# Four tiles open behind a kept layer norm, its scaled chunks in SBUF, and later groups of the multilayer stages tile by tile

## The reference

```python
for i in range(DEPTH_2):                       # 2
    mix = nsa_pool_mixer(...) if i % 2 == 0 else gla_mixer(...)
    x = layer_norm(ALPHA * x + mix, ln1_g[i], ln1_b[i])
    x = layer_norm(ALPHA * x + sqrelu_mlp(x, mlp_w1[i], mlp_w2[i]), ln2_g[i], ln2_b[i])

def layer_norm(x, g, b):
    mu = mean(x); var = mean(square(x - mu))
    return (x - mu) * rsqrt(var + LN_EPS) * g + b

def sqrelu_mlp(x, w1, w2):                     # w1: 1024 x 4096, w2: 4096 x 1024
    return square(relu(x @ w1)) @ w2
```

## Time and profile before

| what | us |
|---|---|
| median of 3 runs | 1947.76 |
| the runs | 1945.41 to 1947.98 |
| the profiled execution, its own time | 1947.59 |
| span of its trace, first to last instruction | 1945.8 |

### The profile page before, as it was taken

One profiled execution on the slowest core, in us unless ns is written; L12 is line 12 of the kernel. 1 busy time (PEld: TensorE's weight loads), 2 busy tenths in 40 slices (PEclk: granted clock), 3 DMA queues, 4 the chain that ended last, 5 costly groups with the idle time before them and its releaser, 6 DMA issues.

```text
span 1945.8 us, 24354 instructions
## 1 busy us (share of the span) xinstructions
PE 1892.9 (97%) x8938; PEld 1516.6 (78%) x8938; DVE 793.7 (41%) x1305; ACT 432.0 (22%) x850; POOL 1071.2 (55%) x622
## 2 busy tenths in 40 slices
PE   7989999999999999999999999999999999999997
PEld 5868787888888888875778888887776778888885
DVE  4965333343342434579451212136523371212126
ACT  4323322310000121045140101023414140101022
POOL 5734663565757656430456665564752446666552
PEclk9989999999999999999999999999999999999998
DMA  5322332222333325210123332222321223332321
GB/s 220 109 65 74 96 102 65 78 96 87 119 98 108 98 84 208 67 55 2 56 76 107 98 97 87 87 95 79 108 87 42 67 75 99 106 99 97 97 87 44
DMA packets 46879, 175.99 MB, mean 90 GB/s; under 512 B 5200, under 2 KB 5328, under 8 KB 46032
## 3 DMA queue, kind: packets, MB, share of 16 engines
q1 hardware_dynamic: 46512, 169.55, 27.0%
q10 hardware_dynamic: 288, 5.31, 0.7%
HBM read 172.74 MB, written 2.10 MB: 90 GB/s over the span
## 4 chain that ended last, share of the span: by engine, by line
PE 94%; DVE 3%; ACT 1%; issue 1%; POOL 0%; DMA 0%; SPq 0%; DVEq 0%; POOLq 0%
PE acc L471 17%; PE acc L473 17%; PE acc L472 17%; PE acc L498 7%; PE acc L494 7%; PE acc L495 7%; PE acc L521 1%; PE acc L522 1%; PE acc L523 1%; PE acc L1052 1%; PE misc L926 1%; PE acc L1054 1%; PE acc L1053 1%; PE acc L542 1%; PE acc L541 1%; PE acc L540 1%
## 5 line engine op out<-in xcount | busy, mean ns | idle before, releaser
L2389 POOL TENSOR_SCALAR w_hi<-raw 128x1024 fp32r<-128x1024 f32 x309 | 331.3, 1072 | 816.8 <-PE acc L498 323.3
L2391 POOL TENSOR_TENSOR w_lo<-raw,w_hi 128x1024 fp32r<-128x1024 f32 x309 | 744.7, 2410 | 25.8
L471 PE MATMUL acc<-x_hi,w_hi 128*128 128x512 f32 x872 | 343.3, 394 | 0.0
L473 PE MATMUL acc<-x_hi,w_lo 128*128 128x512 f32 x872 | 339.6, 389 | 0.0
L472 PE MATMUL acc<-x_lo,w_hi 128*128 128x512 f32 x872 | 339.4, 389 | 0.0
L1790 DVE TENSOR_TENSOR h<-acc,h 128x512 f32<-128x512 f32 x120 | 82.9, 691 | 367.7 <-PE acc L473 234.1
L471 PE MATMUL acc<-y_hi,w_hi 128*128 128x512 f32 x590 | 231.1, 392 | 0.0
L473 PE MATMUL acc<-y_hi,w_lo 128*128 128x512 f32 x590 | 229.6, 389 | 0.0
L472 PE MATMUL acc<-y_lo,w_hi 128*128 128x512 f32 x590 | 229.6, 389 | 0.0
L471 PEld LDWEIGHTS acc<-x_hi,w_hi 128*128 128x128 f32 x872 | 163.8, 188 | 35.4 <-issue 2.3
L473 PEld LDWEIGHTS acc<-x_hi,w_lo 128*128 128x128 f32 x872 | 163.7, 188 | 34.2
(11 more groups left out here) (398 smaller groups left out, 2650.2 us busy)
## 6 DMA issues: line engine op xcount, KB each, us to landing
raw<-weights_dram SPq DMA_DIRECT2D x309, 512.0 KB, 3.5
w_cmp<-w_cmp_dram ACTq DMA_DIRECT2D x1, 4096.0 KB, 14.7
h<-x_dram SPq DMA_DIRECT2D x2, 1024.0 KB, 6.5
out_dram<-h SPq DMA_DIRECT2D x8, 256.0 KB, 2.0
small<-small_dram SPq DMA_DIRECT2D x1, 1408.0 KB, 16.4
small<-small_dram ACTq DMA_DIRECT2D x1, 1088.0 KB, 5.0
mem_in<-mem_dram SPq DMA_DIRECT2D x1, 1024.0 KB, 13.5
const<-const_dram SPq DMA_DIRECT2D x1, 640.0 KB, 9.5
```

What stands on the lines that cost most here:

```text
L471: mm(out, m["w_hi"][:, slot, k], hi[:, k], start=k == 0, stop=False)
L473: last = mm(out, m["w_lo"][:, slot, k], hi[:, k], start=False, stop=k == kc - 1)
L2389: nc.gpsimd.tensor_scalar(hi, m["raw"][:, slot], 1.0, 0.0, ALU.mult, ALU.add).then_inc(sem("weights_high"), 1)
L2391: nc.gpsimd.tensor_tensor(m["w_lo"][:, slot].rearrange("p k n -> p (k n)"), m["raw"][:, slot], bf(hi), ALU.subtract).then_inc(sem("weights ...
```

## The change

Three things are changed. The scaled chunks of the three kept norms go round by three in SBUF (`xs`, in space of scratch tiles) instead of PSUM. Since the fourth result bank is free by that, `four_opening` opens four tiles side by side for the first six chunks, and then finishes them one behind the other, chunks 6 and 7 of each in a row. And the opening is done in the first group of `mlp_a` and `mlp_b` alone: the later groups, whose `x` has long been complete, run all eight `x` tiles with `dense`. For that the first group stands ahead of the loop, which runs groups 1 and 2.

```diff
+    place("xs", [3, S], F32, arena - 4 * 4 * S)
...
+        if name in KEPT:
+            return self.misc[:, 2], self.misc[:, 1], [self.m["xs"][:, b] for b in range(3)]
...
     def opening(t0, first_tile, norm):
+        if norm in KEPT:
+            four_opening(t0, first_tile, norm)
+            return
         opening_of(t0, first_tile, x_hi, x_lo, "norm_high", "norm_ready", chunks_before(norm))
-        if norm in KEPT:
-            pe.wait_ge(sem("norm_kept"), KC * (KEPT.index(norm) + 1))
+
+    def four_opening(t0, first_tile, norm):
+
+        slots = [(first_tile + j) % RING for j in range(RING)]
+        before = chunks_before(norm)
+        for j in range(RING - 1):
+            claim(t0 + j)
+        for k in range(KC - 2):
+            pe.wait_ge(sem("norm_high"), before + k + 1)
+            for j, slot in enumerate(slots):
+                if k == 0 and j == RING - 1:
+                    claim(t0 + j)
+                mm(acc[:, slot], m["w_hi"][:, slot, k], x_hi[:, k], start=k == 0, stop=False)
+                mm(acc[:, slot], m["w_lo"][:, slot, k], x_hi[:, k], start=False, stop=False)
+            pe.wait_ge(sem("norm_ready"), before + k + 1)
+            for slot in slots:
+                mm(acc[:, slot], m["w_hi"][:, slot, k], x_lo[:, k], start=False, stop=False)
+        for slot in slots:
+            for k in range(KC - 2, KC):
+                pe.wait_ge(sem("norm_ready"), before + k + 1)
+                mm(acc[:, slot], m["w_hi"][:, slot, k], x_hi[:, k], start=False, stop=False)
+                mm(acc[:, slot], m["w_lo"][:, slot, k], x_hi[:, k], start=False, stop=False)
+                last = mm(acc[:, slot], m["w_hi"][:, slot, k], x_lo[:, k], start=False, stop=k == KC - 1)
+            last.then_inc(sem("tile_done"), 1)
+        pe.wait_ge(sem("norm_kept"), KC * (KEPT.index(norm) + 1))
...
-        for i in range(3 if norm else 0, n):
+        for i in range(RING if norm in KEPT else 3 if norm else 0, n):
...
-    def mlp_group(name, g, norm, high, next_norm=None):
+    def mlp_group(name, g, norm, high, next_norm=None, first=False):
         t0 = g * 16 + START[name]
-        opening(t0, START[name], norm)
-        for j in range(3, 8):
+        if first:
+            opening(t0, START[name], norm)
+        for j in range(RING if first else 0, 8):
             dense(t0 + j, (START[name] + j) % RING, x_hi, x_lo)
...
     def mlp(name, norm, high, next_norm):
-        with pe.Fori(0, GROUPS - 1) as g:
+        mlp_group(name, 0, norm, high, first=True)
+        with pe.Fori(1, GROUPS - 1) as g:
             mlp_group(name, g, norm, high)
         mlp_group(name, GROUPS - 1, norm, high, next_norm)
```

## The result

The change makes the kernel slower, a little: 1949.68 us median of 19 runs (1948.09 to 1952.62), against 1947.3 us of the kernel before in 19 runs beside it (1945.34 to 1948.4). The medians lie 2.4 us apart. The ratio that the runs give is 1.0014, with a 95% interval of 1.0008 to 1.002, or 2.7 us (1.6 to 3.9). I had forecast 1947.0 and no change that can be measured; the time lies above my range.

What follows compares the result with a forecast made beforehand. TensorE was taken as the bound, busy for 1892.9 of 1945.8 us. Terms of -1.08, +0.06 and 2 x 0.17 made -0.7 us, from 1947.59 to 1946.9, and with the median's 0.17 to 1947.0; range 1944.6 to 1949.2.

Steps and rivals of the forecast that it cites:

- Four tiles instead of three: In three openings: the wait for chunk 0's low half and its restart go, 0.36 us a norm, 1.08 us gained.
- Scaled chunks in SBUF: Behind each kept norm: `x_hi` of chunk 0 comes 0.02 us later, 0.06 us in all.
- Shared reads in the openings: In the openings: low halves with two SBUF inputs meet no split, as GpSimd is idle; cost nothing.
- Ending one behind the other, the fifth tile in the `mlp` stages: In `mlp_a` and `mlp_b`: TensorE waits for the fifth tile's split, 0.09 us plus 0.08 of restart, 0.17 each.
- Later groups: In the `mlp` stages: running later groups tile by tile keeps the same products and pitch; value 0.
- the jump into the loop: In the `mlp` stages: entering the loop between running tiles costs 0, bounds 0 and 0.6 us for each of two.
- Behind `ln2a`: In `gla_in`: a gate product longer than the 0.09 us lateness stands before the fifth tile, so the cost is 0.
- which wait anyway: In the later groups: tiles ending earlier help GpSimd, ScalarE and VectorE, said to be waiting anyway; no size given.
- slower, by the shared reads: In the openings: low halves take 2.6 us instead of 0.65, costing 13.5 us a norm, about 1988 us; chance 0.03.
- The forecast's last step: For the whole kernel: from 1946.9 us after the change, with the median 0.17 above the profiled execution, to 1947.0 us.

Runs made afterwards that it cites:

- e3: The kernel before, with only `tile_done` of `gla_in`'s three opening tiles raised later, after 6, 12 and 18 products of the fourth tile; 1951.18 us, ratio 1.0021.
- e4: The changed kernel with gate values of `gla_in` that VectorE reads put into free PSUM banks; 1945.63 us, ratio 0.9994 to the kernel before.

## Why the prediction was wrong, step by step

- *Four tiles instead of three.* Right. TensorE has no wait for the low half of chunk 0, and 96 products take 21.85 us: 96 x 0.2267 = 21.76 and 0.08 for the first. VectorE's pitch of 1.91 us a chunk, which I read from the first chunks, falls to 1.3 from the fifth on, so the cover was larger still.
- *Scaled chunks in SBUF*, the 0.02 us of `x_hi`. Right: TensorE idles 0.65 us instead of 0.62, and ScalarE's `x_hi` takes 36 ns longer (724 against 688).
- *Shared reads in the openings*, costed at nothing. Right for the openings: GpSimd is idle for 22 us and the low half takes 745 ns, as before.
- *Ending one behind the other, the fifth tile in the `mlp` stages.* Mis-sized. I had 0.09 us late and 0.08 of restart, 0.17. The split was done when I said, and TensorE went on without a gap:

```profile
1002.08 1.06 POOL L2420 TENSOR_SCALAR w_hi<-raw 128x1024 fp32r<-128x1024 f32 x1 [21.98 <-PE acc L509]
1003.22 2.40 POOL L2422 TENSOR_TENSOR w_lo<-raw,w_hi 128x1024 fp32r<-128x1024 f32 x1
```

```profile
1005.57 0.39 PE L509 MATMUL acc<-x_lo,w_hi 128*128 128x512 f32 x1
1005.79 0.40 PE L474 MATMUL acc<-x_hi,w_hi 128*128 128x512 f32 x1
```

  The split ends at 1003.22 + 2.40 = 1005.62, and the fifth tile's first product starts at 1005.79, on the pitch. The 0.26 us from a split to a product came from an engine that had stood still; in flow, with no idle time of TensorE ahead, 0.17 was enough. So the `mlp` stages gained 0.30 and 0.37, not 0.17.
- *Later groups*, 0, *and the jump into the loop*, 0. Right: the pitch goes on across it.

```profile
1070.88 0.39 PE L476 MATMUL acc<-y_hi,w_lo 128*128 128x512 f32 x1
1071.11 0.39 PE L474 MATMUL acc<-x_hi,w_hi 128*128 128x512 f32 x1
```

- *Behind `ln2a`: 0.* This is the step that failed. I asked only whether the fifth tile's split would be in time for TensorE, and it was. I did not follow the split to its other effect. I had the price of a collision in hand, 4.67 us against 2.48 for four operations of the same form, and a rule for it, and looked for VectorE's operations with two SBUF inputs only where the diff adds them. `gla_in` has 24 of its own, on a chain of four heads that was 3.0 us from being asked for. In my own sum the splits that lie ahead of that chain came 1.4 us later, and I priced the move as a matter between GpSimd and TensorE alone. What the runs showed in its place: +4.1 us in that stage (e3, 239.56 against 235.49) for three signals that come later, by way of a `k_g` that is 5.5 us late in e3 and 5.2 in the change.
- The sentence that tiles that end earlier help engines "which wait anyway" was of the same kind. An idle engine that starts its work at another moment can stretch the work of a second one, as the scan of 3.30 us for 1.22 shows.
- Of the rivals, "slower, by the shared reads" had the mechanism and the wrong place: it put the collisions into the openings, and gave itself 0.03.
- The forecast's last step is off by a rounding: 1947.59 - 0.68 + 0.17 is 1947.1, not 1947.0. It changes nothing.

In sum: +4.1 in `gla_in`, and -0.31, -0.30 and -0.37 for the three openings, +3.1 us by the distances, against 2.7 (1.6 to 3.9) by the times. The gains in the openings came for the reasons forecast; the one term that decided the sign had been put at nothing.

The Trainium skill (SBUF — State Buffer, section Who interferes with whom) says that a VectorE instruction with two SBUF inputs contends with a GpSimd instruction that reads SBUF, and one with at most one SBUF input, outside VectorE's 2-port performance modes, does not. The traces here agree: the scan takes 3.30 us beside a split, and 1.22 beside one with one input in PSUM (e4). The same section of the Trainium skill adds that the order of issue decides who blocks, and both sides are seen here, the scan's 3.30 and the `w_hi` of 1.95.

Why head 1 is the one that loses most (3.9 of the 5.2 us; head 0 loses 1.4) is argued from two traces and not shown by a run of its own: by 42.4 to 42.8 us behind the mark GpSimd is paced by TensorE again, in both kernels. VectorE starts head 1 at 41.0 us before and at 42.4 after, late by what head 0 lost to the moved splits, and so right on a split instead of ahead of it.

## What to carry to other kernels

When a change moves a signal, follow it to every engine that wakes by it, and from there to the operations of other engines that then run beside it; the idle engine's moment of work can be what matters, not its length. Where a chain has many operations with two SBUF inputs beside a busy GpSimd, read its slack before touching any order near it, and put one input into a free PSUM bank: here the last `k_g` then came at 70.85 or 71.19 us wherever the splits lay (first one from 14.08 to 18.51). And compare stages by distances between marks in the trace: they repeated to 0.1 us where the times of one kernel spread over 2 to 5.

## What the runs showed that I had not expected

- A scan from SBUF with two inputs, 1.22 us alone, took 3.30 beside a split; the time of a collision can fall on it as on any tensor operation.
- GpSimd's split stretched as well, `w_lo` from 2.40 to 2.71 us and `w_hi` from 1.05 to 1.95, so a collision also shifts the next split. The kernel before has this too.
- A wait of 2.4 us of TensorE was followed by a granted clock of 0.50 from 1420 to 1423, and what ran then took 1.5 us more than in the kernel before. The 0.6 us of idle time behind each norm cost no such thing: the products behind them have the pitch of 0.23 us from the second on.
